# Moving softmax maxima and sums between row and column by DMA through DRAM, in the mixing stage of a hybrid DeltaNet and forgetting-attention layer

## The reference

```python
cum = jnp.cumsum(jnp.moveaxis(log_f, 2, 1), axis=-1)
for i in range(s // Q_BLOCK):
    lo, hi = i * Q_BLOCK, (i + 1) * Q_BLOCK
    logits = (jnp.einsum('bhqd,bhkd->bhqk', q[:, :, lo:hi], k[:, :, :hi]).astype(jnp.float32) * scale
              + cum[:, :, lo:hi, None] - cum[:, :, None, :hi])
    logits = jnp.where(s_pos[None, :] <= t_pos[:, None], logits, -jnp.inf)
    p = jax.nn.softmax(logits, axis=-1)
    outs.append(jnp.einsum('bhqk,bhkd->bhqd', p.astype(v.dtype), v[:, :, :hi]))
y_b = o_b.reshape(b, s, FOX_WIDTH) * jax.nn.silu(z_b)
```

## Time and profile before

| | |
|---|---|
| median of 3 runs | 1731.47 us (1729.21 to 1731.8) |
| the profiled execution: its own time | 1733.44 us |
| the profiled execution: span of its instructions | 1731.3 us |
| mean granted TensorE clock | 0.966 |

### The profile page before, as it was taken

One profiled execution on the slowest core, in us unless ns is written; L12 is line 12 of the kernel. 1 busy time (PEld: TensorE's weight loads), 2 busy tenths in 40 slices (PEclk: granted clock), 3 DMA queues, 4 the chain that ended last, 5 costly groups with the idle time before them and its releaser, 6 DMA issues. The chain is left out here.

```text
span 1731.3 us, 22970 instructions
## 1 busy us (share of the span) xinstructions
PE 1635.6 (94%) x8226; PEld 1271.2 (73%) x8226; DVE 919.5 (53%) x1427; ACT 691.7 (40%) x1307; POOL 649.6 (38%) x578
## 2 busy tenths in 40 slices
PE   7999999999999999999389999999999999959998
PEld 5888888888788888888256666766666676637886
DVE  7365555554286673011345655664666656433855
ACT  0446363635111113111036565655665666730100
POOL 1212121212211111110247776866776877810211
PEclk9999999999999999999579998999999999969999
DMA  6225252525933332224823534442644432062742
GB/s 234 71 91 164 74 160 74 158 73 144 118 128 120 120 120 79 73 79 119 216 68 101 131 90 119 133 107 77 169 132 116 125 92 75 18 215 61 219 134 85
DMA packets 183572, 202.66 MB, mean 117 GB/s; under 512 B 45380, under 2 KB 129092, under 8 KB 180420
## 3 DMA queue, kind: packets, MB, share of 16 engines
q1 hardware_dynamic: 182148, 196.16, 40.0%
q10 hardware_dynamic: 1312, 5.05, 0.8%
HBM read 125.92 MB, written 75.24 MB: 116 GB/s over the span
## 5 line engine op out<-in xcount | busy, mean ns | idle before, releaser
L507 PE MATMUL bank<-x_hi,w_hi 128*128 128x512 f32 x992 | 394.7, 398 | 3.6 <-DVEq L801 3.6
L1404 POOL TENSOR_TENSOR m_p_lo<-m_p,m_p_hi 128x512 fp32r<-128x512 f32 (+1 forms) x320 | 365.1, 1160 | 85.1 <-ACT m_p_hi L1360 80.9
L507 PE MATMUL bank<-x_hi,w_lo 128*128 128x512 f32 x992 | 388.5, 392 | 0.0
L507 PE MATMUL bank<-x_lo,w_hi 128*128 128x512 f32 x992 | 387.6, 391 | 0.0
L1358 ACT ACTIVATE m_p<-m_st,m_fcol 128x512 f32<-128x512 f32 (+1 forms) x320 | 203.7, 637 | 239.4 <-PE m_st L1234 127.8
L532 POOL TENSOR_TENSOR w_lo<-w_raw,w_hi 128x512 fp32r<-128x512 f32 x66 | 97.6, 1500 | 496.9 <-ACT w_hi L588 496.9
L1467 DVE TENSOR_REDUCE m_maxima<-m_aux 128x1 f32<-128x512 f32 (+2 forms) x320 | 196.7, 621 | 143.4 <-PE m_aux L1207 93.9
L507 PEld LDWEIGHTS bank<-x_hi,w_hi 128*128 128x128 f32 x992 | 187.0, 189 | 39.9 <-issue 4.0
L507 PEld LDWEIGHTS bank<-x_hi,w_lo 128*128 128x128 f32 x992 | 186.7, 188 | 39.7
L507 PEld LDWEIGHTS bank<-x_lo,w_hi 128*128 128x128 f32 x992 | 187.0, 189 | 36.7
L1360 ACT ACTIVATE m_p_hi<-m_st,m_fcol 128x512 fp32r<-128x512 f32 (+1 forms) x320 | 202.0, 631 | 0.0
(11 more groups left out here) (191 smaller groups left out, 2497.0 us busy)
## 6 DMA issues: line engine op xcount, KB each, us to landing
w_raw<-in_w SPq DMA_DIRECT2D x31, 512.0 KB, 3.9
dram_feat<-ring SPq DMA_DIRECT2D x48, 256.0 KB, 3.3
arena<-dram_gates SPq DMA_DIRECT2D x32, 256.0 KB, 4.9
m_K<-dram_k_hi SPq DMA_DIRECT2D x16, 512.0 KB, 7.3
m_Q<-dram_q_hi SPq DMA_DIRECT2D x64, 128.0 KB, 4.4
o_y<-dram_mixT SPq DMA_DIRECT2D x16, 512.0 KB, 6.1
o_x<-in_x SPq DMA_DIRECT2D x16, 512.0 KB, 4.1
out<-o_res SPq DMA_DIRECT2D x15, 512.0 KB, 5.0
```

The lines of the kernel that those rows point to most:

```text
L507: mm = pe.matmul(banks[bank_of(s)][:], w[:, i % 2, k * P:(k + 1) * P], x[:, k, b * BLOCK:(b + 1) * BLOCK], start=(k == 0 and n == 0), stop ...
L1404: pool.tensor_tensor(p_lo[(s - 1) % PL][:, off:], p[(s - 1) % PL][:, off:], p_hi[(s - 1) % PH][:, off:].bitcast(F32), ALU.subtract).then_i ...
```

## The change

Two conversions between a row and a column leave TensorE and GpSimd.

**Row maxima**, for groups 4 to 31 (`ROWS_ON_PE = 4`): VectorE negates `mcol` into `neg_max`; SP stores it, 4 bytes at a time, as a row in DRAM one slot after the group's last `max`, and loads the row into `Q2` six slots after it. TensorE waits for that load at the group's start. `row` is gone from TensorE, GpSimd and VectorE for these 28 groups.

**Softmax sums**, for groups 0 to 30: SP spreads `den` over 64 partitions (slot +1 behind `finish`), VectorE takes the reciprocal there (+6), SP stores it to DRAM (+7) and loads it back, broadcast to 64 partitions (+11), VectorE rescales (+16), SP stores `yb` (+17). `sum` and `scale` stay for group 31 alone. `gated` has four buffers in place of two.

```diff
 SUM_AFTER, SCALE_AFTER = 2, 5
-END_SLOT = N_UNITS + LAG + SCALE_AFTER
+SPREAD, INVERT, GATHER, SPREAD_BACK, RESCALE = 1, 6, 7, 11, 16
+ROWS_ON_PE = 4
+END_SLOT = N_UNITS + LAG + SCALE_AFTER + 2
...
-        put(min(slot_of(n - 1) + 2, first_unit(G) - 1) if G else -1, ("row", G))
-        put(last_unit(G) + LAG + SUM_AFTER, ("sum", G))
-        put(last_unit(G) + LAG + SCALE_AFTER, ("scale", G))
+        if G < ROWS_ON_PE:
+            put(min(slot_of(n - 1) + 2, first_unit(G) - 1) if G else -1, ("row", G))
+        if G == N_GROUPS - 1:
+            put(last_unit(G) + LAG + SUM_AFTER, ("sum", G))
+            put(last_unit(G) + LAG + SCALE_AFTER, ("scale", G))
...
                     for G in range(N_GROUPS):
-                        if G + 2 < N_GROUPS and s == ROW_SLOT[G] + 1:
+                        done_at = last_unit(G) + LAG
+                        if G >= ROWS_ON_PE and s == MAX_SLOT[G] + 1:
+                            sp.wait_ge(neg_max_ready, G - ROWS_ON_PE + 1)
+                            sp.dma_start(max_rows[G].rearrange("(a p) -> p a", p=P), neg_max[:].bitcast(F32), allow_slow_non_contiguous=True)\
+                              .then_inc(max_row_stored, 16)
+                        if G >= ROWS_ON_PE and s == MAX_SLOT[G] + 6:
+                            sp.wait_ge(max_row_stored, 16 * (G - ROWS_ON_PE + 1))
+                            sp.wait_ge(scores_ready, last_unit(G - 4) + 1)
+                            sp.dma_start(Q2[G % 4][FD:FD + 1, :].bitcast(F32), max_rows[G:G + 1]).then_inc(max_row_landed[G % 4], 16)
+                        if G < N_GROUPS - 1 and s == done_at + SPREAD:
+                            sp.wait_ge(den_ready, G + 1)
+                            sp.dma_start(dens[G % 2][:], den[G % 2][:].rearrange("o (p j) -> o p j", j=512 // FD))\
+                              .then_inc(dens_landed[G % 2], 16)
+                        if G < N_GROUPS - 1 and s == done_at + GATHER:
+                            sp.wait_ge(recs_ready, G + 1)
+                            sp.dma_start(rec_rows[G].rearrange("(p j) -> p j", j=512 // FD), recs[G % 2][:]).then_inc(recs_stored, 16)
+                        if G < N_GROUPS - 1 and s == done_at + SPREAD_BACK:
+                            sp.wait_ge(recs_stored, 16 * (G + 1))
+                            sp.dma_start(rec_b[G % 2][:], rec_rows[G:G + 1].broadcast_to([FD, 512])).then_inc(rec_b_landed[G % 2], 16)
+                        if G + 2 < N_GROUPS and s == MAX_SLOT[G] + 2:
                             sp.wait_ge(mcol_ready, G + 1)
                             load_max_queries(G + 2)
...
-                        pe.wait_ge(row_ready, G + 1)
+                        if G < ROWS_ON_PE:
+                            pe.wait_ge(row_ready, G + 1)
+                        else:
+                            pe.wait_ge(max_row_landed[G % 4], 16 * (G // 4))
...
+                def invert(G):
+                    dve.wait_ge(dens_landed[G % 2], 16 * (G // 2 + 1))
+                    if G >= 2:
+                        dve.wait_ge(recs_stored, 16 * (G - 1))
+                    dve.reciprocal(recs[G % 2][:], dens[G % 2][:]).then_inc(recs_ready, 1)
+
+                def rescale(G):
+                    dve.wait_ge(rec_b_landed[G % 2], 16 * (G // 2 + 1))
+                    if G >= 2:
+                        dve.wait_ge(yb_stored[G % 2], 16 * (G // 2))
+                    dve.scalar_tensor_tensor(yb[G % 2][:], gated[G % 4][:], 0.5, rec_b[G % 2][:], ALU.mult, ALU.mult)\
+                       .then_inc(yb_ready, 1)
```

More of the change, by code:

```diff
@@ L979 @@
 AUX_INDEX = {x: n for n, x in enumerate(AUX)}
-ROW_SLOT = {item[1]: s for s in AUX_AT for item in AUX_AT[s] if item[0] == "row"}
+MAX_SLOT = {item[1]: s for s in sorted(AUX_AT) for item in AUX_AT[s] if item[0] == "max"}
 def unit(s):
@@ L1028, in mix @@
         max_diag = sb("max_diag", [P, 4, P], F32R)
-        den = sb("den", [1, 512])
+        neg_max = sb("neg_max", [P, 4], F32R)
+        den = [sb(f"den{i}", [1, 512]) for i in range(2)]
+        dens, recs = ([sb(f"{n}{i}", [FD, 512 // FD]) for i in range(2)] for n in ("dens", "recs"))
+        rec_b = [sb(f"rec_b{i}", [FD, 512]) for i in range(2)]
         rcol = sb("rcol", [P, 4])
         rec_diag = sb("rec_diag", [P, 4, P])
-        gated = [sb(f"gated{i}", [FD, 512]) for i in range(2)]
+        gated = [sb(f"gated{i}", [FD, 512]) for i in range(4)]
         yb = [sb(f"yb{i}", [FD, 512]) for i in range(2)]
@@ L1071, in mix @@
              "ya_ready"))
+        neg_max_ready, max_row_stored, recs_ready, recs_stored = (sem(n) for n in (
+            "neg_max_ready", "max_row_stored", "recs_ready", "recs_stored"))
+        max_row_landed, dens_landed, rec_b_landed = sems("max_row_landed", 4), sems("dens_landed", 2), sems("rec_b_landed", 2)
+        max_rows = nc.dram_tensor("dram_max_rows", (N_GROUPS, 512), F32).ap()
+        rec_rows = nc.dram_tensor("dram_rec_rows", (N_GROUPS, 512), F32).ap()
         za_of = scr["feat"][ZA_T:ZA_T + GH].rearrange("t p (c s) -> c p t s", s=P)
@@ L1216, in do_aux @@
                         for a in range(4):
-                            mm = pe.matmul(b[:, a:a + 1], den[:, a * P:(a + 1) * P], ones[0:1, 0:1], start=True, stop=True)
+                            mm = pe.matmul(b[:, a:a + 1], den[what[0] % 2][:, a * P:(a + 1) * P], ones[0:1, 0:1], start=True, stop=True)
                     else:
-                        pe.wait_ge(rec_diag_ready, what[0] + 1)
+                        pe.wait_ge(rec_diag_ready, 1)
                         mm = pe.matmul(b[0:FD, :], ones[:], flat(rec_diag[:]), start=True, stop=True)
@@ L1386, in do_aux @@
                     G = what[0]
-                    if kind == "max" and what[1] == 3 and what[2] == G % NB:
+                    if kind == "max" and what[1] == 3 and what[2] == G % NB and G < ROWS_ON_PE:
                         done(pool, row_ready, G - 1)
@@ L1469, in do_aux @@
                             dve.wait_ge(aux_used, m + 1)
[L1470 removed]
+                            done(dve, max_diag_ready, min(G - 1, ROWS_ON_PE - 1))
                             dve.reduce_max(mcol[:], maxima[:, :, 0:g + 1], AX.X).then_inc(mcol_ready, 1)
+                            if G >= ROWS_ON_PE:
+                                dve.wait_ge(mcol_ready, G + 1)
+                                if G > ROWS_ON_PE:
+                                    dve.wait_ge(max_row_stored, 16 * (G - ROWS_ON_PE))
+                                dve.tensor_scalar(neg_max[:], mcol[:].bitcast(F32), -1.0, None, ALU.mult).then_inc(neg_max_ready, 1)
                     elif kind == "row":
                         G = what[0]
[L1474 to L1475 removed]
                         came()
@@ L1554, in _ @@
                         finish(*unit(s - LAG)[0:2])
+                    for G in range(N_GROUPS - 1):
+                        if s == last_unit(G) + LAG + INVERT:
+                            invert(G)
+                        if s == last_unit(G) + LAG + RESCALE:
+                            rescale(G)
                     for item in AUX_AT.get(s, ()):
```

19 lines of the change are left out of this document (9 added, 10 removed).

## The result

The kernel became slower: 1837.1 us in the median (1834.2 to 1844.4, 4 runs) beside 1731.6 us before (1729.2 to 1740.6, 4 runs), a ratio of 1.0605 [1.0556, 1.0655], or 105.5 us. The profiled execution took 1838.5 us with a span of 1836.0, 104.7 more than before's 1731.3.

What follows compares the result with a forecast made beforehand. TensorE's time was taken to bound each slot of `mix`: 1733.4 - 70 (work removed) + 59 (stalls) + 16 (clock) = 1738.4 us for the profiled execution, a median of about 1737 us, range 1708 to 1762.

Steps and rivals of the forecast that it cites:

- The step that failed: The store of the maxima was likened to the chunk's m_XT load: 0.53 us of issue, 2.3 us to landing.
- Place and mechanism of the stalls: TensorE waits for the row at the starts of groups 7, 11, ..., 31, 59 us in all.
- With every landing at 5 us: Upper figure for the seven stalls at group starts, if each row landing took 5 us: 72 us.
- Groups of 4, 8 and 12 units have cover enough: At these starts 3 slots or more (6 us) remain for a landing of 2.3 to 4.4 us.
- VectorE's new waits at 0 to 5 us: VectorE's waits in `invert` or `rescale` for the sums' DMAs: costed at nothing, range 0 to 5 us.
- a sign of being wrong: Main step wrong if the seven waits are missing or below 5 us, or VectorE's DMA waits hold the auxiliary banks.
- TensorE's work, 70 us: Gain from the `sum`, `scale` and `row` products leaving TensorE: 70 us, up to 80 allowed.
- The distances: Time from each removed TensorE product to the next instruction, taken as its cost: 67.8 us together.
- the busy times, 65.8: Busy times of the removed TensorE product groups, 33.2 and 32.6 us, taken as the bound from above for overlap.
- The clock, 16 us: Loss from TensorE at half speed behind five long new stalls: 16 us, between 0 and 25.
- The rule named in the prediction: A strided last dimension becomes one descriptor per element; transfers under 512 B are read, modified and written.
- Rival 3: Longer stalls: small stores hold queues, SP falls behind, VectorE stands in `invert` or `rescale`; 1770 us, chance 0.19.

Runs made afterwards that it cites:

- kernel 3: The changed kernel with the maxima stored as 128 pieces of 16 bytes, not 512 of 4, row out of order: 1737.4 us beside 1732.3, ratio 1.0031.
- kernel 8: The changed kernel with two buffers for `neg_max`, stores and their order kept: 1836.1 us beside 1733.5, ratio 1.059.
- kernel 5: The changed kernel with 16-byte pieces and the row loaded two slots earlier for groups of 16 units, row out of order: 1684.1 us beside 1733.5.
- kernel 1: The changed kernel with the row maxima back on TensorE for all groups, sums still by DMA: 1674.9 us beside 1732.3, ratio 0.967.
- kernel 11: The changed kernel with its 512 pieces of 4 bytes set 512 bytes apart in DRAM, SP's order kept: 1753.5 us beside 1735.2, ratio 1.009.
- kernel 9: As kernel 5, but the row's load restores the right order by reading 512 pieces of 4 bytes: 1725.0 us beside 1735.2, ratio 0.9928.

## Why the prediction was wrong

It was wrong in size, by 100 us and outside its range of 1708 to 1762; the side (slower) was right, at a chance of 0.46.

- **The step that failed** is "I take the store as like it, since five slots lie between store and load": the store taken as the m_XT load, 2.3 us. It takes 8.2 to 14.8, and while it is out the DMAs around it are held. The sum had one landing of the row in each stall and nothing for the store. Two ways from there to TensorE are seen: SP stands 52.4 us at the landing of the reciprocals' store (15.8 in kernel 3), with all behind it late, and the row's own load lands late, after 8.1 us at group 7. Kernel 3, whose store lands in 1.9 us, gives 1737.4 us, the forecast's 1737, and stalls of 11.9, 12.1, 9.7, 11.1, 6.0, 5.7 and 3.1 us at the seven starts, 59.6 together; the prediction had 13.5, 13.6, 7.5, 10.4, 7.3, 7.3 and 3.4, or 63 together, and 59 without the 3.8 that group 15 had already (gone in kernel 3, as the prediction said, so its new stalls are 56). So with the store priced rightly the working stands, and the 100 us are that step.
- **Place and mechanism of the stalls: right.** Seven groups of 16 units, ended by the row's DMA, behind the next group's store, the broadcast and the queries in SP's order. Moving the load out of that order takes 53 us more off kernel 3 (1737.4 to 1684.1).
- **Bounds.** With every landing at 5 us the prediction's own terms come to 68 or 70 us, not the 72 it gives; nothing else was worked out from it.
- **Groups of 4, 8 and 12 units have cover enough: wrong** with this store (6.2 and 5.2 us at groups 6 and 10, 16 us in all), right with 16-byte pieces (60.1 us of waits, 59.6 of them at the seven).
- **VectorE's new waits at 0 to 5 us: wrong.** 37.5 us for `dens` and 24.6 for the store. The latter cost nothing of their own (kernel 8); the former fit the 15.1 us more ahead of `max`, which the prediction had named as a sign of being wrong ("if VectorE's new waits on DMAs hold the auxiliary banks").
- **TensorE's work, 70 us: low.** Kernel 5 has 78.9 us less at almost the same clock, and kernel 1, where 61.4 was counted for the sums alone, 1635.6 - 1564.8 = 70.8 less, of which 57.4 reached the end. The distances missed some 10 us, and the busy times, 65.8, were no bound from above: beside them the `max` products, which follow the removed ones, are busy 126.7 us in kernel 1 in place of 133.3.
- **The clock, 16 us: too little for these stalls, too much for those forecast.** At the same instructions TensorE is busy 1585.4 us in the kernel after and 1556.7 in kernel 5: 29 us. Kernel 3, with stalls as forecast, has 1567.8, or 11. These two, 14 us together, should have made kernel 3 faster than forecast. Its profiled execution has the same span as before's (1731.2 and 1731.3): busy time -67.8, waits for the row +60.1, ahead of the low values' product +3.6, ahead of `max` -1.1, so about 5 us lie in smaller groups, and its median is another 3.7 above that execution. That the total met the forecast is in part luck; the stalls met it one by one, within 2.2 us.
- **The rule named in the prediction** (the Trainium skill, "DMA: Bandwidth & Descriptors", Rules for kernel authors and Specifications) warned of the right transfer. One descriptor for each element does not by itself decide: kernel 11 has as many elements and is 84 us faster. That transfers under 512 B are read, modified and written would fit neighbours that share a block of DRAM, but no run here shows such a read, and size alone does not decide either: 128 packed pieces of 16 bytes land in 1.4 us at best where 128 of 4 take 7.9.
- **Rival 3**, "small stores hold the queues", stood at 1770 us and a chance of 0.19. It had the mechanism first in its list and at a third of its price: it counted 3 us more a stall, and the seven show 8, with 16 us at other groups.

What stays open: what holds the other DMAs is only known from outside. The runs show that it depends on the distance of the addresses, that it crosses queues, and, at the one place looked at, that the engines show no bytes for most of it; that several writes to one block wait for each other is an explanation that fits, not one that was seen. That kernel 9 loses its 41 us by reading small pieces is argued from its one difference to kernel 5.

The best kernel of all is kernel 1, 3.3% faster than before: the sums through DRAM, where the hops have slots to spare, and the maxima on TensorE, where their product costs 0.23 us and TensorE waits 0.6 us in all at the groups' starts.

## What to carry to other kernels

A column stored as a row in DRAM is not a small DMA because it is 2 KB: look at how far apart in DRAM the pieces lie that different partitions write, and price the DMAs around it too. What was fast here were pieces of 16 bytes in a row (1.9 us in the median), the reciprocals' of 32 (1.7 in kernel 1), and pieces of 4 bytes set 64 or more apart (2.0 to 2.5). Replace an engine's product by a trip through DRAM only where its result has slack; 31 trips with slots to spare gained 57 us here; 28 lost 128, seven of them with a start right behind, and 16-byte pieces took back 100 of the 105 us that the whole change lost. And read a late load in the order of the engine that issues it: two slots earlier in that order were worth 53 us beside a fast store and 39 beside the slow one.

## What was unexpected of the hardware

- 512 pieces of 4 bytes side by side in DRAM landed in 8.2 to 14.8 us; 8 bytes apart in 4.2 at best and 4.6 in the median, 16 apart in 2.5 and 4.7, 32 apart in 1.8 and 4.3, 64 to 512 apart in 1.8 and 2.0 to 2.5. 128 pieces of 4 bytes side by side still took 7.9 to 14.2, and 128 pieces of 16 bytes 1.4 at best and 1.9 in the median.
- While such a store is out, other DMAs are late whichever engine issued it: the landing of `m_QM` went from 4.0 to 8.4 us in the median (9.5 with the store on ScalarE's queue, 3.9 with 16-byte pieces), and a 2 KB store of reciprocals beside it took 8.7, with the DMA engines showing no bytes for the last 5 us of it, and landed within 0.4 us of the store ahead of it.
- A stall of 21 us is followed by TensorE at a granted clock of 0.55 over the next 4 us, nearer to 1.2 than to 2.4 GHz; over the whole stretch, with 170 of 735 us idle, the clock was 0.87 where it had been 0.98.
